# Attention units kept one more deep in flight in a two-block transformer kernel

## What is computed

```
for l in range(DEPTH_2):                                   # 2 layers
    xn = rmsnorm_2(x, norm_mix[l])
    (qa, ka, va, qb, kb, vb, qc, kc, vc, qi, ki, wi, gates) = jnp.split(xn @ w_in[l], offsets, axis=-1)
    o_a = chunk_band_attention(qa, ka, va, rel_bias_a[l])              # 8 heads of 64
    o_b = diff_attention(apply_rope(qb), apply_rope(kb), vb, lam, lam_init, subln_b[l])
    o_c = dsa_attention(apply_rope(qc), apply_rope(kc), vc,            # top-k keys by an index score
                        apply_rope(qi), apply_rope(ki), wi * H_IDX ** -0.5, topk)
    g = jax.nn.sigmoid(gates).reshape(b, s, 3, D_MODEL)
    y = g[:, :, 0] * (o_a @ w_up_a[l]) + g[:, :, 1] * (o_b @ w_up_b[l]) + g[:, :, 2] * (o_c @ w_up_c[l])
    x = x + y @ w_out[l]
    x = x + memory_cross_attention(rmsnorm_2(x, norm_cross[l]), mem_n, w_q_x[l], w_kv_x[l], w_o_x[l])
    x = x + swiglu(rmsnorm_2(x, norm_ffn[l]), w_gu[l], w_down[l])
```

## Time and profile before

| | |
|---|---|
| median of three runs | 1640.3 us |
| the profiled execution | 1638.12 us |
| its span, first to last instruction | 1636.1 us |
| TensorE matmul busy | 1562.6 us, 96% |
| VectorE busy | 893.3 us, 55% |
| ScalarE busy | 651.5 us, 40% |
| granted TensorE clock, mean | 0.983 |

### The profile page before, as it was taken

One profiled execution on the slowest core, in us unless ns is written; L12 is line 12 of the kernel. 1 busy time (PEld: TensorE's weight loads), 2 busy tenths in 40 slices (PEclk: granted clock), 3 DMA queues, 4 the chain that ended last, 5 costly groups with the idle time before them and its releaser, 6 DMA issues.

```text
span 1636.1 us, 25662 instructions
## 1 busy us (share of the span) xinstructions
PE 1562.6 (96%) x10931; PEld 1255.8 (77%) x10931; DVE 893.3 (55%) x1302; ACT 651.5 (40%) x1022; POOL 62.6 (4%) x30
## 2 busy tenths in 40 slices
PE   8998989889989999999999999999999999999998
PEld 7886434434435349988889799999989889899998
DVE  6933212112111148667887576647566879576654
ACT  2034112112201126454764554435454664464443
POOL 0000000000000000024000000000007000000000
PEclk9988999999999999999999999999999999999999
DMA  9165999999999995626334566474634543265550
GB/s 350 49 252 206 417 428 428 428 428 429 429 429 427 427 402 199 206 104 199 136 117 142 165 196 197 165 259 157 210 122 156 180 155 130 85 215 190 181 205 28
DMA packets 126913, 393.79 MB, mean 241 GB/s; under 512 B 4320, under 2 KB 60000, under 8 KB 114016
## 3 DMA queue, kind: packets, MB, share of 16 engines
q1 hardware_dynamic: 126816, 392.38, 63.5%
HBM read 386.34 MB, written 1.05 MB: 237 GB/s over the span
## 4 chain that ended last, share of the span: by engine, by line
PE 73%; DVE 12%; DMA 10%; ACT 2%; issue 1%; SPq 0%; DVEq 0%; ACTq 0%
PE psum L1259 11%; PE psum L990 10%; PE psum L991 10%; PE psum L993 10%; DMA ring<-w 8%; PE psum L1324 4%; DVE outs L1984 3%; PE psum L1596 2%; PE psum L1594 2%; DVE w_lo L636 2%; PE psum L1597 2%; PE psum L1222 2%; PE psum L1417 1%; PE psum L1418 1%; PE psum L1416 1%; PE psum L951 1%
## 5 line engine op out<-in xcount | busy, mean ns | idle before, releaser
L990 PE MATMUL psum<-h_parts,w_hi 128*128 128x256 f32 x1472 | 358.2, 283 | 0.1
L991 PE MATMUL psum<-h_parts,w_lo 128*128 128x256 f32 x1472 | 352.5, 279 | 0.0
L636 DVE TENSOR_TENSOR w_lo<-raw_a,w_hi 128x1024 fp32r<-128x1024 f32 x184 | 221.9, 1222 | 114.7 <-ACT w_hi L1616 114.0
L990 PEld LDWEIGHTS psum<-h_parts,w_hi 128*128 128x128 f32 x1472 | 276.3, 188 | 6.1 <-issue 5.4
L991 PEld LDWEIGHTS psum<-h_parts,w_lo 128*128 128x128 f32 x1472 | 277.2, 188 | 0.2
L1616 ACT ACTIVATE w_hi<-raw_a 128x1024 fp32r<-128x1024 f32 x202 | 210.4, 1055 | 160.1 <-PE psum L993 62.7
L993 PE MATMUL psum<-h_parts,w_hi 128*128 128x256 f32 x1472 | 201.9, 279 | 0.0
L1259 PE MATMUL psum<-ring,outs 128*64 128x512 f32 x720 | 167.2, 621 | 26.0 <-DMA ring<-w 24.8
L993 PEld LDWEIGHTS psum<-h_parts,w_hi 128*128 128x128 f32 x1472 | 184.7, 188 | 0.0
L1259 PEld LDWEIGHTS psum<-ring,outs 128*64 128x64 f32 x720 | 58.5, 143 | 132.0 <-issue 132.0
L1616 ACT ACTIVATE w_hi<-raw_b 128x1024 fp32r<-128x1024 f32 x100 | 104.8, 1056 | 90.4 <-PE psum L993 52.7
(11 more groups left out here) (310 smaller groups left out, 2535.0 us busy)
## 6 DMA issues: line engine op xcount, KB each, us to landing
ring<-w SPq DMA_DIRECT2D x76, 2048.0 KB, 16.4
raw_a<-w_in SPq DMA_DIRECT2D x20, 2048.0 KB, 7.9
raw_a<-w_gu SPq DMA_DIRECT2D x32, 1024.0 KB, 7.8
raw_b<-w_in SPq DMA_DIRECT2D x10, 2048.0 KB, 8.9
wp<-w SPq DMA_DIRECT2D x8, 2048.0 KB, 18.7
hs<-w SPq DMA_DIRECT2D x8, 2048.0 KB, 23.1
raw_b<-w_gu SPq DMA_DIRECT2D x12, 1024.0 KB, 7.6
raw_a<-w_down SPq DMA_DIRECT2D x8, 1536.0 KB, 6.6
```

Source lines behind the costliest of these rows:

```text
L636: return eng.tensor_tensor(chunk_part(w_lo, n), chunk_raw(n), chunk_part(w_hi, n).bitcast(F32), ALU.subtract)
L990: mm(to, hi[:, k, :], h_hi[:, k, :], start=(k == 0), stop=False)
L991: mm(to, lo[:, k, :], h_hi[:, k, :], start=False, stop=False)
```

## The change

The slots of an attention are laid out anew. In slot s TensorE does the first 12 products of the gate chunk (`gates_head`, six of its eight k, high and low weights), the apply of s-3, the other 12 products, scores of s and the turn of s-2. For ScalarE and VectorE the order in a slot is probs s-1, exp s-1, the copy of output s-3, the weight split, scores s, the low part, the copy of transposes s-2; the splits of a slot are placed at a marker (`here`) and run one chunk further ahead than before. The two tail units of each attention are written out in `WORK`: index product 0 goes between turn 6 and apply 6, product 1 between turn 7 and apply 7, and both Relus are one step of ScalarE; after C the first quarter of up 0 (`up_head`, 24 products) goes between turn 23 and apply 23, and the subln sums go ahead of apply 22. The up projections, the subln sums and the outputs get other seats in PSUM. The number of products, copies and waits is the same.

```diff
+GATE_HEAD = 6
@@ attention
-    for s in range(first, last + 2):
-        if first <= s - 1 < last:
-            steps.append(("probs", s - 1))
-        steps += extra.get(s, [])
+    for s in range(first, last + 1):
+        if s > first:
+            steps += [("probs", s - 1), ("exp", s - 1)]
+        done = [("apply", s - 3)] if s - 3 >= first else []
+        for w in extra.get(s, []):
+            if w[0] == "gates":
+                steps += [("gates_head",) + w[1:]] + done + [("here",), w]
+                done = None
+            else:
+                steps.append(w)
+        if done is not None:
+            steps += done + [("here",)]
         if s < last:
             steps.append(("scores", s))
         steps += behind.get(s, [])
-        if first <= s - 1 < last:
-            steps.append(("turn", s - 1))
-        if first <= s - 2 < last:
-            steps.append(("apply", s - 2))
-        if s < last:
-            steps.append(("exp", s))
+        if s - 2 >= first:
+            steps.append(("turn", s - 2))
@@ WORK
-        + [("index_product", 0), ("index_product", 1), ("apply", 7)]
+        + [("index_product", 0), ("apply", 6), ("turn", 7), ("index_product", 1), ("apply", 7)]
...
-        + [("subln_sums",), ("apply", 23), ("outs_high", 2), ("outs_low", 2), ("subln",), ("subln_rest",), ("up", 16, 0),
+        + [("subln_sums",), ("apply", 22), ("turn", 23), ("up_head", 16, 0), ("apply", 23), ("outs_high", 2), ("outs_low", 2), ("subln",), ("subln_rest",), ("up", 16, 0),
@@ with_splits
-        for _ in range({"subln_sums": used + PARTS - split, "subln_rest": 1}.get(w[0], 0)):
+        for _ in range({"up_head": used + PARTS - split, "subln_rest": 1}.get(w[0], 0)):
@@ DUO_OF
-DUO_OF = {"p_vb": 3, "p_idx": 2, "i_0": 2, "i_1": 0, "p_qc": 3, "p_kc": 1, "p_vc": 0, "u_24": 1, "u_25": 2, "u_26": 0, "u_27": 3}
+DUO_OF = {"p_vb": 3, "p_idx": 2, "i_0": 2, "i_1": 0, "p_qc": 3, "p_kc": 1, "p_vc": 0, "subln": 0, "up_0_0": 3, "up_0_1": 1, "up_2_0": 0, "up_2_1": 2, "up_1_0": 3, "up_1_1": 1,
+          "out_0": 0, "out_1": 1, "u_24": 1, "u_25": 2, "u_26": 0, "u_27": 3}
@@ tensor: split_chunk in two
+            def chunk_head(i, o, to, l, ks):
                 n = SPLIT_THROUGH[i] - chunks_of(LAYER_PIECES[i]) + o
-                parts_ready(pe, n, l)
+                if ks.start == 0:
+                    parts_ready(pe, n, l)
                 hi, lo = chunk_part(w_hi, n), chunk_part(w_lo, n)
-                for k in range(KD):
+                for k in ks:
                     mm(to, hi[:, k, :], h_hi[:, k, :], start=(k == 0), stop=False)
                     mm(to, lo[:, k, :], h_hi[:, k, :], start=False, stop=False)
+
+            def split_chunk(i, o, to, l, first=0):
+                chunk_head(i, o, to, l, range(first, KD))
+                hi = chunk_part(w_hi, SPLIT_THROUGH[i] - chunks_of(LAYER_PIECES[i]) + o)
                 for k in range(KD):
                     last = mm(to, hi[:, k, :], h_lo[:, k, :], start=False, stop=(k == KD - 1))
@@ tensor: up
-                        for q in range(4):
+                        for q in (range(0, 1) if kind == "up_head" else range(int(b == 0), 4)):
@@ scalar
-                    elif kind == "index_product":
-                        t = 1 - w[1]
-                        nk = P * (t + 1)
+                    elif w == ("index_product", 1):
                         act_e.wait_ge(idx_done, l * 2 + 2)
-                        logits = view(duo(f"i_{t}"), 0, 4, SEQ)[:, :, 0:nk]
-                        f(logits, logits, ACT.Relu, scale=SCALE).then_inc(relu_ready, 1)
+                        for t in (1, 0):
+                            logits = view(duo(f"i_{t}"), 0, 4, SEQ)[:, :, 0:P * (t + 1)]
+                            f(logits, logits, ACT.Relu, scale=SCALE).then_inc(relu_ready, 1)
```

More of the change, by code:

```diff
@@ L164, in gate_parts @@
     return {s + o: [("gates", piece + i, gate + i, o)] for i, s in enumerate(starts) for o in range(4)}
-def without_last(steps, step):
-    assert steps[-1] == step
-    return steps[:-1]
 WORK = ([("norm", "mix"), ("lam",), ("proj", 0, "qa"), ("proj", 1, "ka"), ("proj_v", 2, "va"),
@@ L174 @@
          ("proj_v", 5, "vb"), ("rope", 1, "kb"), ("index_proj", 6), ("evac", 2, "idx")]
-        + without_last(attention(0, 8, {**gate_parts((1, 5), 7, 0), 1: [("gates", 7, 0, 0), ("index_weights",)],
-                                        4: [("gates", 7, 0, 3), ("rope", 2, "idx")]}), ("apply", 7))
-        + [("index_product", 0), ("index_product", 1), ("apply", 7)]
+        + attention(0, 8, {**gate_parts((1, 5), 7, 0), 1: [("gates", 7, 0, 0), ("index_weights",)],
+                                        4: [("gates", 7, 0, 3), ("rope", 2, "idx")]})
+        + [("index_product", 0), ("apply", 6), ("turn", 7), ("index_product", 1), ("apply", 7)]
         + [("index", 1), ("index", 0), ("proj", 9, "qc"), ("proj", 10, "kc"), ("evac", 3, "qc"), ("evac", 4, "kc"),
            ("proj_v", 11, "vc")]
-        + without_last(attention(8, 24, {**gate_parts((9, 13, 17, 21), 12, 2),
+        + attention(8, 24, {**gate_parts((9, 13, 17, 21), 12, 2),
                                          19: [("outs_high", 0), ("gates", 14, 4, 2)], 20: [("gates", 14, 4, 3), ("square_b",)]},
-                                  {13: [("rope", 3, "qc")], 14: [("rope", 4, "kc")], 19: [("outs_low", 0)]}), ("apply", 23))
-        + [("subln_sums",), ("apply", 23), ("outs_high", 2), ("outs_low", 2), ("subln",), ("subln_rest",), ("up", 16, 0),
+                                  {13: [("rope", 3, "qc")], 14: [("rope", 4, "kc")], 19: [("outs_low", 0)]})
+        + [("subln_sums",), ("apply", 22), ("turn", 23), ("up_head", 16, 0), ("apply", 23), ("outs_high", 2), ("outs_low", 2), ("subln",), ("subln_rest",), ("up", 16, 0),
            ("gate_last",), ("outs_high", 1), ("outs_low", 1), ("up", 17, 2), ("up", 18, 1)]
@@ L200, in with_splits @@
     for w in work:
-        used += {"proj": 4, "proj_v": 4, "up": 4, "out": 4, "gate_up": 4, "gates": 1, "down": 1, "index_proj": 3, "cross_q": 1}.get(w[0], 0)
-        unit = w[0] in ("scores", "probs", "turn", "apply", "gates", "exp", "square_b")
+        used += {"proj": 4, "proj_v": 4, "up": 4, "out": 4, "gate_up": 4, "gates_head": 1, "down": 1, "index_proj": 3, "cross_q": 1}.get(w[0], 0)
+        unit = w[0] in ("gates_head", "here", "scores", "probs", "turn", "apply", "gates", "exp", "square_b")
         if w == ("norm", "mix") and layer == 0:
@@ L239, in with_splits @@
             low = []
-        held = w[0] in ("gates", "probs", "scores", "turn", "apply", "cross_q", "square_b", "sums", "evac", "rope", "index_product", "subln_sums", "outs_high", "outs_low", "subln", "subln_rest") or (w[0] == "exp" and w[1] >= 24)
-        for _ in range({"subln_sums": used + PARTS - split, "subln_rest": 1}.get(w[0], 0)):
+        held = w[0] in ("gates_head", "up_head", "gates", "probs", "scores", "turn", "apply", "cross_q", "square_b", "sums", "evac", "rope", "index_product", "subln_sums", "outs_high", "outs_low", "subln", "subln_rest") or w[0] == "exp"
+        for _ in range({"up_head": used + PARTS - split, "subln_rest": 1}.get(w[0], 0)):
             out += [("split", split), ("low", split)]
@@ L295, in tenants @@
             names.append(f"i_{w[1]}")
-        elif kind == "gates":
+        elif kind == "gates_head":
             names += [f"g_{w[2]}"] if w[3] == 0 and w[2] in (0, 2) else []
@@ L1444, in _ @@
                         i, g, o = w[1], w[2], w[3]
+                        split_chunk(i, o, duo("g_0" if g < 2 else "g_2")[:, o * SEQ:(o + 1) * SEQ], l, GATE_HEAD)
+                    elif kind == "gates_head":
+                        i, g, o = w[1], w[2], w[3]
                         name = "g_0" if g < 2 else "g_2"
@@ L1449, in _ @@
                             enter(pe, name, l)
-                        split_chunk(i, o, duo(name)[:, o * SEQ:(o + 1) * SEQ], l)
+                        chunk_head(i, o, duo(name)[:, o * SEQ:(o + 1) * SEQ], l, range(GATE_HEAD))
                     elif kind == "scores":
```

3 lines of the change are left out of this document (1 added, 2 removed).

## The result

The changed kernel takes 1642.41 us, the median of 20 executions (1641.02 to 1647.02), beside 1639.78 us for the kernel before on the same chips (20 executions, 1637.16 to 1641.49). The ratio is 1.0021, 95% interval 1.0014 to 1.0027: 2.3 to 4.4 us slower (the medians differ by 2.6 us, the means by 3.4). Forecast were 1646.1 us, or 5.8 us slower. The profiled execution took 1642.42 us, 4.3 more than that of before (1638.12).

The account below looks back on a forecast made before the run. TensorE was taken to bound the kernel, except behind output 23, where VectorE's list does. Attention A +0.7, B and C -0.2, end of C +2.4 make 2.9 us a layer, +5.8 in two: 1646.1 us, range 1635 to 1650.5.

Parts of the forecast that it names:

- D: Rival: the split costs 0.29 and delayed copies build on each other; +5 us a layer, 1650.5 us; chance 0.10.
- The end of C: From the end of the last gate chunk to the end of output 23: 6.4 us for 4.0, +2.4 a layer.
- TensorE waiting for the low part: In the up chunks: low part ready 14.4 us after output 23, TensorE there at about 11.5 and waiting.
- 40.3 us from its end to the first product of out's second half: Stretch after output 23: claimed to stay 40.3 us, with VectorE working without pause.
- all of it hangs on output 23: After C: VectorE's list up to out's second half, 40.3 us, follows only from the end of output 23.
- Attention A: First attention stretch: stalls +0.7, split +0.1, end +0.3, about 0.4 absorbed; +0.7 us a layer.
- B and C: Second attention stretch to its last gate chunk: stalls -2.1+1.2, split +1.1, turn 22 moved -0.4; -0.2 us a layer.
- the split chunk in the B slots: Each split chunk costs 0.20 us; in the 8 B units the removed boundary gives back 0.08.
- The stalls: Second attention stretch: turn waits of 2.1 us go, scores wait 1.75 us for PSUM pairs, of which 1.2 kept.
- A (all stalls go): Rival: all turn waits go for nothing, the quarter costs 2.4 us; -1.4 us a layer, 1637.5 us; chance 0.18.
- B: Rival: stalls go, VectorE's list doesn't hold the end, quarter fills TensorE's time; -4.4 us a layer, 1631.5 us; chance 0.12.
- C: Rival: the stalls move but the quarter is free; +0.5 us a layer, 1641.3 us; chance 0.10.

## Why the prediction was right, and where its steps were off

The forecast had the sign, the mechanism and the range; the size was 5.8 us for a measured 2.6 by the medians and 3.4 by the means (interval 2.3 to 4.4), and 4.6 by the stage. The range, 1635 to 1650.5, was wide enough to hold no change as well, so that the time fell into it says little. There is some luck in the sum too: the attentions came out 1.3 us a layer lower than forecast and the stretches behind output 23 0.7 higher. (In the rivals, D's 5 us a layer give 1650.3, not 1650.5.)

**The end of C** was the heart of it, and it held: 6.42 us from the last gate chunk to the end of output 23 (6.4 forecast), VectorE's list without a pause but for 0.42 us, TensorE waiting for the low part inside the up chunks until 14.5 us after output 23 (14.4 forecast). Both runs that undo it, by the quarter's place and by the root's, win back 2.7 and 2.8 us a layer of 3.1 (the last three rows of the first table), and the same quarter alone in the kernel before loses 2.7 us a layer, 2.2 up to the end of output 23 and 0.5 behind it with the fall of the clock.

*"40.3 us from its end to the first product of out's second half"* was 40.81. I had let TensorE wait there for nothing, and the wait itself did cost nothing: where the clock didn't fall behind it, the stretch stayed at 40.3 us. The term that I had at nothing without a reason was the clock. I had read it as 1.00 in the attentions of the kernel before and not asked what a new wait of 2.6 us would do to it. It fell behind this wait in both layers, the up chunks ran late, a rounding came 0.42 us late for VectorE, and the stretch took 0.5 us more. The statement that *all of it hangs on output 23* was right for this order of ScalarE's queue only; the run with the root first showed that only the queue, not the data, made it so.

**Attention A** came to +0.35 in place of +0.7: output 0 waited 1.46 us (1.5 forecast) and scores 5 1.54 (1.85), 0.3 us less than walked, and scores 3 did not wait (0.2 forecast). The mechanism was read correctly from the queue: turns wait for nobody, copies behind exp and Tanh take their place, and moving only those behind the copy removed the waits of the scores.

**B and C** came to -1.13 in place of -0.2, the largest miss of a term. The stalls were well sized: scores 15, 16 and 17 waited 0.08, 0.54 and 0.55, 1.17 us in all for 1.2 forecast. What was too dear was the split chunk in the B slots, together with the boundary that it takes away. The changed kernel's timeline shows a chunk's two pieces around an output product, from start to start: in A 1.57 and 1.60 us, in B 1.49 and 1.58, 3.17 and 3.07 in sum.

```profile
703.10 0.36 PE L992 MATMUL psum<-h_parts,w_hi 128*128 128x256 f32 x1
...
704.67 0.66 PE L1508 MATMUL psum<-wp,vals 128*64 128x128 f32 x8
705.26 0.39 PE L992 MATMUL psum<-h_parts,w_hi 128*128 128x256 f32 x1
...
706.86 0.49 PE L1477 MATMUL psum<-qk 64*128 64x128 f32 x4
```

```profile
775.37 0.36 PE L992 MATMUL psum<-h_parts,w_hi 128*128 128x256 f32 x1
...
776.86 0.61 PE L1501 MATMUL psum<-wp,vals 128*128 128x128 f32 x4
777.22 0.36 PE L992 MATMUL psum<-h_parts,w_hi 128*128 128x256 f32 x1
...
778.80 0.49 PE L1477 MATMUL psum<-qk 64*128 64x128 f32 x4
```

Against 3.00 the split costs 0.17 us in A, and 0.07 in B, or 0.09 against a chunk between B units of the kernel before (2.98 us); I took 0.20 for both. Two B slots, from scores to scores, show the whole balance, first before, then after:

```profile
774.43 0.70 PE L1467 MATMUL psum<-qk 64*128 64x256 f32 x4
...
782.39 0.70 PE L1467 MATMUL psum<-qk 64*128 64x256 f32 x4
```

```profile
774.54 0.70 PE L1477 MATMUL psum<-qk 64*128 64x256 f32 x4
...
782.52 0.70 PE L1477 MATMUL psum<-qk 64*128 64x256 f32 x4
```

7.96 us have become 7.98: split less boundary is 0.01 us a slot, where I had 0.20 less 0.08. Over eight B slots that is 0.9 us, the size of the miss. The Trainium skill, TensorEngine Tiling (Array Packing), Key Properties, says that it is a change of tiling mode that drains the engine. B's output product has the shape of the chunk's products (128 x 128) and pays the small price (0.07 to 0.09 us), A's and C's (128 x 64) the larger one (0.17 us), so the trace agrees; I had weighed this page against a flat 0.20 and kept the flat number for the B slots, which had no such row.

**The median.** The stage lost 4.6 us in two layers, the median 2.6. With the quarter alone it was 5.4 and 2.2, with the root early and old seats 3.9 and 0.5 in the first profile; the versions without the 1.83 or 2.6 us wait have medians 0.5 to 2.7 us below what their stages say. The part of an execution outside the stages varies too: its start, and the falls in the cross attention, 1 to 3 us each. In the fourteen profiles there is one in 2 of the 11 layers whose stage had a fall, and in 8 of the 17 others. If that is more than chance, a kernel whose stage has the falls is spared some of those behind it, and the medians move less than the stages; 28 layers don't decide it, and no run tested it. It isn't settled.

**Rivals.** A (all stalls go) is out: scores wait. B and C (the quarter is free) are out in the form they had, by the quarter runs; it becomes free only once the root no longer waits for output 23. D's dearer split is out.

## What to carry to other kernels

Work that one engine does early is free only if nobody's list starts behind it: before moving independent work ahead of a step, ask which other engine's unbroken list begins with that step's result, and in which order a third engine's queue hands it over. Here one place in ScalarE's order decided about 6 us in the changed kernel and 2 to 4 in the kernel before, once the PSUM seats allowed it. When the pipeline is made deeper the waits for data turn into waits for buffers, and the copies that free buffers belong ahead of the long functions in the same queue. For effects under 0.2% compare one stage in the trace, with the granted clock beside it: where the clock did the same the stage repeated to about 0.1 us, where the whole execution spread over 4.

## What the runs showed of the hardware

- A wait of TensorE of 1.83 to 2.6 us was followed by a granted clock of 0.50 for 3.3 us and a little more, in some executions and layers and not in others: in 8 of 10 cases behind 2.6 us, in 3 of 4 behind 1.83 us and in 10 of 28 behind the 1.85 us of the cross attention. The fall began between a few tenths of a microsecond before the wait's end and 1.7 us after it. It cost 0.4 to 0.5 us behind the wait of 2.6 us, 1.5 us behind that of 1.83 us, and 1.0 to 1.6 us in the cross attention, or 2.7 to 3.0 where it lasted double. Waits of 1.56 us and less were followed by no such stretch in the attentions and the up projections of any profile here. The Trainium skill, TensorE: Matmul & The Clock Gate, Part 1, describes the observation of the engine's activity as running freely, so that its moment doesn't follow the kernel; that the same wait was followed by a fall in layer 1 and not in layer 0 agrees with it.
- One excursion more from a run of the chunk's products to 128 x 64 products and back costs 0.17 us (a split chunk 3.17 us against 3.00), to 128 x 128 ones and back 0.09 us (3.07 against 2.98).
